# Start, end of the scan and entry to the feed-forward in another order; scan levels 0 to 7 as 64 by 64 blocks

## The reference

```
x = x + rmsnorm(concat(att, rec) @ w_out)      att: 8 query heads, 2 key heads, rope; rec: gated scan, 4 heads, 2 directions
x = x + rmsnorm(cross_attention(rmsnorm(x), rmsnorm(mem)) @ w_xo)
x = x + rmsnorm(conv_ffn(rmsnorm(x)))          width 2816, a convolution over 3 rows
x = x + rmsnorm((sig(ga) * (diff_attention @ A) + sig(gb) * (mla_attention @ B)) @ w_o)
x = x + rmsnorm((silu(h @ w_gate) * (h @ w_up)) @ w_down)
```

## Time and profile before

| | us |
|---|---|
| median of 3 runs | 932.08 (931.82 to 932.86) |
| the profiled execution | 931.06 |
| its span in the trace | 929.3 |
| PE busy | 896.8 |
| DVE busy | 616.0 |
| ACT busy | 479.0 |
| POOL busy | 79.9 |

### The profile page before, as it was taken

One profiled execution on the slowest core, in us unless ns is written; L12 is line 12 of the kernel. 1 busy time (PEld: TensorE's weight loads), 2 busy tenths in 40 slices (PEclk: granted clock), 3 DMA queues, 4 the chain that ended last, 5 costly groups with the idle time before them and its releaser, 6 DMA issues.

```text
span 929.3 us, 13932 instructions
## 1 busy us (share of the span) xinstructions
PE 896.8 (97%) x5540; PEld 794.2 (85%) x5540; DVE 616.0 (66%) x969; ACT 479.0 (52%) x841; POOL 79.9 (9%) x118
## 2 busy tenths in 40 slices
PE   5999899999989999999999999999999999999997
PEld 5988797889868999999878788788888789999996
DVE  5777977574668767668667747676787673654643
ACT  5844356564458346446535356675474672424331
POOL 1300200010020000000114210012011200000000
PEclk9999999999999999999999999999999999999999
DMA  9544324352538334655445455243255574564531
GB/s 339 188 136 148 124 92 163 109 204 95 181 128 300 136 137 145 217 183 194 170 148 185 177 181 182 73 164 139 91 187 176 168 262 136 176 204 165 181 137 45
DMA packets 91696, 152.56 MB, mean 164 GB/s; under 512 B 1968, under 2 KB 52272, under 8 KB 91376
## 3 DMA queue, kind: packets, MB, share of 16 engines
q1 hardware_dynamic: 91232, 150.94, 47.1%
...
q10 hardware_dynamic: 288, 0.47, 0.2%
...
## 4 chain that ended last, share of the span: by engine, by line
PE 81%; DVE 9%; ACT 4%; issue 3%; DMA 2%; POOL 0%; DVEq 0%; POOLq 0%; SPq 0%; ACTq 0%
PE ps L541 71%; DVE sb_wlo L2033 2%; DMA sb_ring<-in_w_in 2%; ACT sb_whi L1485 1%; PE ps L866 1%; PE ps L713 1%; PE ps L699 1%; PE ps L663 1%; PE ps L962 1%; PE ps L769 1%; PE ps L1137 1%; DMA sb_x<-in_x 1%; DVE sb_b L2186 1%; ACT sb_probs L1737 0%; DVE sb_b L2161 0%
## 5 line engine op out<-in xcount | busy, mean ns | idle before, releaser
L2033 DVE TENSOR_TENSOR sb_wlo<-sb_ring,sb_whi 128x1024 fp32r<-128x1024 f32 (+2 forms) x169 | 201.8, 1210 | 108.6 <-ACT sb_whi L1485 108.1
L1485 ACT ACTIVATE sb_whi<-sb_ring 128x1024 fp32r<-128x1024 f32 (+2 forms) x169 | 173.4, 1043 | 106.0 <-PE ps L541 99.5
L541 PE MATMUL ps<-sb_whi,sb_tbhi 128*128 128x512 f32 (+2 forms) x296 | 116.7, 394 | 2.8 <-DVE sb_wlo L2033 2.8
L541 PE MATMUL ps<-sb_whi,sb_tblo 128*128 128x512 f32 (+2 forms) x296 | 113.5, 383 | 0.0
L541 PE MATMUL ps<-sb_wlo,sb_tbhi 128*128 128x512 f32 (+2 forms) x296 | 113.5, 383 | 0.0
L541 PE MATMUL ps<-sb_whi,sb_tahi 128*128 128x512 f32 (+1 forms) x180 | 69.4, 386 | 0.7 <-DVE sb_wlo L2033 0.6
L541 PEld LDWEIGHTS ps<-sb_whi,sb_tbhi 128*128 128x128 f32 x296 | 55.7, 188 | 14.9 <-DVE sb_wlo L2033 4.6
L541 PE MATMUL ps<-sb_wlo,sb_tahi 128*128 128x512 f32 (+1 forms) x180 | 67.3, 374 | 0.0
L541 PE MATMUL ps<-sb_whi,sb_talo 128*128 128x512 f32 (+1 forms) x180 | 67.2, 374 | 0.0
L541 PEld LDWEIGHTS ps<-sb_whi,sb_tblo 128*128 128x128 f32 x296 | 55.6, 188 | 10.7
L541 PEld LDWEIGHTS ps<-sb_wlo,sb_tbhi 128*128 128x128 f32 x296 | 55.7, 188 | 9.2
...
## 6 DMA issues: line engine op xcount, KB each, us to landing
...
```

What stands on the lines that cost most here:

```text
L541: mm = pe.matmul(o, l[a_], r[b_], start=(start and n == 0), stop=(stop and n == 2), skip_group_check=not check)
L1485: act.activation(piece_pair(m)[0], src, ACT.Copy).then_inc(s("hi_done"), 1)
L2033: dve.tensor_tensor(low, pieces[m][1], high.bitcast(F32), ALU.subtract).then_inc(s("lo_done"), 1)
```

## The change

- **Beginning and pre_x_g.** Instead of the diagonal matrices DVE scales the rows themselves, in four instructions of 128x512, and PE transposes them (16 transposes). At the beginning POOL makes the inverse root of each row block apart, the four scalings are waited for in pairs of tiles, the first weight transfer holds 128 columns instead of 256, and PE first runs four matmuls on a zeroed buffer. The memory's norm scales in four instructions too.
- **Scan.** Levels 0 to 7 compute only the blocks on the diagonal of 64 by 64: 16 matmuls of 64x64 a level, the first half of the rows into PSUM partitions 0 to 63 and the second into 64 to 127. The kept matrix has 128x256 numbers a bank instead of 128x512, and so have the masked copies; the masks shrink from 896 to 384 columns. Level 7's block is the off-diagonal one; ACT puts it, and the compact matrix, in place in six copies after level 6 (which DVE waits for at level 8).
- **End of the scan.** DVE goes on to level 6 and 7 before the rotation of row block 0. The rotation of row block 1 (four products and two sums) moves to POOL.
- **Entry to the feed-forwards.** The low pieces stand before or behind the scalings in another order, the two scalings of row block 0 come together, the tiles of block 0 ahead of the squares of block 1.
- **Smaller ones.** POOL's inverse root per row block multiplies the first square in before the second is there. One or two low pieces move at three places (w_out's residual, "va0", the attentions' limit); in `attend` the values of head n-2 are taken before the other work, and `normalise_oa(1)` goes from n = 0 to n = 1. The load of one row of gains moves ahead by one chunk.

The diff, cut to its core:

```diff
-            def turn_norm(name, src):
-                pe.wait_ge(s(f"{name}_diag"), R)
+            def turn_norm(name):
+                pe.wait_ge(s(f"{name}_scaled"), 2 * R)
                 for m in range(4):
...
+                    turn(f"{name}.{m}", rows, [2 * m, 2 * m + 1], M[m], 2)
+            pe.wait_ge(s("blank"), 1)
+            for cols in (512, 512, 512, 256):
+                pe.matmul(bank[G[3]][:, 0:cols], probs[:, 0, 0:P], probs[:, 0, 0:cols], start=True, stop=True)
...
+            for r in range(R):
+                for m in range(4):
+                    if m % 2 == 0:
+                        pe.wait_ge(s("pre_mix_g_scaled"), 2 * r + m // 2 + 1)
...
-            def halves(T, h, head, r):
+            def halves(T, h, at):
...
-                        if n == 0:
-                            l, rhs = kdiag[:, at:at + P], hq[:, at:at + P]
-                        elif n < LEVELS:
-                            h = 1 << (n - 1)
-                            l, rhs = keys_at[n % 2][:, at:at + P], halves(QD, h, head, r)
...
+                        for a_ in range(2):
+                            block = slice(a_ * BLOCK, (a_ + 1) * BLOCK)
+                            own_at, other_at = at + a_ * BLOCK, at + (1 - a_) * BLOCK
+                            keys = kdiag if n == 0 else keys_at[n % 2]
+                            if n == 0:
+                                rhs = hq[:, own_at:own_at + BLOCK]
+                            elif n < LEVELS - 1:
+                                rhs = halves(QD, 1 << (n - 1), own_at)
+                            else:
+                                rhs = QD[:, (1 - a_) * NS + other_at:(1 - a_) * NS + other_at + BLOCK]
+                            mm = pe.matmul(bank[M[b]][block, j * BLOCK:(j + 1) * BLOCK], keys[:, own_at:own_at + BLOCK], rhs,
+                                           start=True, stop=True, skip_group_check=True)
...
+            pe.wait_ge(s("scan_blocks"), 2)
...
             def rstd_rows(name, r):
-                pool.wait_ge(s(f"{name}_sq"), 2 * (r + 1))
...
-                step(pool.tensor_tensor(m, m, more, ALU.add))
+                pool.wait_ge(s(f"{name}_sq"), 2 * r + 1)
                 step(pool.tensor_scalar(m, m, 1.0 / D, EPS, ALU.mult, ALU.add))
+                pool.wait_ge(s(f"{name}_sq"), 2 * (r + 1))
+                step(pool.tensor_scalar(m, more, 1.0 / D, m, ALU.mult, ALU.add))
...
+            z, t = qkv[:, 1, 0:640], rtmp[:, 640:1280]
+            zp, tp = (v.rearrange("p (i two) -> p i two", two=2) for v in (z, t))
+            for src, dst, tables in ((z, t, (tsq, tsk)), (z, z, (tcq, tck))):
+                for table, lo, n in zip(tables, (0, 512), (8, 2)):
+                    q = slice(lo, lo + 64 * n)
+                    pool.tensor_tensor(heads(dst[:, q]), heads(src[:, q]), table[:, 1:2, :].to_broadcast([P, n, 64]),
+                                       ALU.mult).then_inc(s("rope1_mul"), 1)
+            pool.wait_ge(s("rope1_mul"), 4)
+            for a_, b_ in ((0, 1), (1, 0)):
+                pool.tensor_tensor(zp[:, :, a_], zp[:, :, a_], tp[:, :, b_], ALU.add).then_inc(s("rope1_added"), 1)
...
+            for half in range(2):
+                for b in range(2):
+                    act.wait_ge(*banks.empty(f"level6.{b}"))
+                block = slice(half * BLOCK, (half + 1) * BLOCK)
+                act.activation(Adiag[block, :, block], Ablock[block, :, :], ACT.Copy).then_inc(s("scan_blocks"), 1)
...
-                        dve.copy_predicated(Adiag[:, 4 * b:4 * b + 4, :],
-                                            masks[:, n - 1:n, :].bitcast(I32).to_broadcast([P, 4, P]),
+                        dve.copy_predicated(Ablock[:, 4 * b:4 * b + 4, :],
+                                            masks[:, n - 1:n, :].bitcast(I32).to_broadcast([P, 4, BLOCK]),
...
             def next_level(n):
-                ahead(reached[f"level{n}"] + 1)
+                if n < 6:
+                    ahead(reached[f"level{n}"] + 1)
                 if 0 < n < LEVELS:
                     double_queries(n - 1)
-                keep_level(n)
+                if n != LEVELS - 1:
+                    keep_level(n)
+                if n >= 6:
+                    ahead(reached[f"level{n}"] + 1)
                 if n < LEVELS - 1:
                     double_keys(n)
...
             ahead(reached["level5"] + 2)
+            next_level(6)
+            ahead(reached["level6"] + 2)
             rope1_turn(0)
-            next_level(6)
+            ahead(reached["level6"] + 3)
+            next_level(7)
             rope1_scale(0)
-            rope1_turn(1)
-            next_level(7)
             rope1_scale(1)
...
-                ahead_of(q1, 3)
-                scaled(post, f"{q0}.0", 0, 0, loads)
                 ahead_of(q1, 4)
                 ahead_of(in0, 1)
+                scaled(post, f"{q0}.0", 0, 0, loads)
                 scaled(post, f"{q1}.0", 1, 0, loads)
                 added_rows(post, (f"{q0}.0", f"{q1}.0"), 0)
-                ahead_of(in0, 2)
                 norm_rows(norm, f"{post}_added", 0)
+                ahead_of(in0, 3)
                 for half in range(2):
                     tiles_lo(norm, T, gain, 0, half)
+                ahead_of(in0, 4)
+                ahead_of(in1, 1)
                 scaled(post, f"{q0}.1", 0, 1, loads)
-                ahead_of(in0, 4)
                 scaled(post, f"{q1}.1", 1, 1, loads)
-                ahead_of(in1, 1)
                 added_rows(post, (f"{q0}.1", f"{q1}.1"), 1)
...
+            ahead_of("va0", 1)
             take_gained("ckvT", ckvT, [0, 1], COL_KVA)
...
-                   {0: [(take_v, 1), (normalise_oa, 1)], 2: [(oaT_lo, 1)], 5: [(take_a, 0, 0)], 6: [(take_a, 0, 1)],
-                    9: [(take_a, 1, 0), (take_a, 1, 1)]})
+                   {0: [(take_v, 1)], 1: [(normalise_oa, 1)], 2: [(oaT_lo, 1)], 5: [(take_a, 0, 0)], 6: [(take_a, 0, 1)],
+                    9: [(take_a, 1, 0), (take_a, 1, 1)]}, pieces_of["w_proj_b_20"][0] + 2)
```

134 lines of the change are left out of this document (74 added, 60 removed).

## The result

The changed kernel takes 916.15 us (median of four runs, 915.11 to 916.60) against 931.95 for the kernel before in the same session: 15.8 us less, a ratio of 0.9827 (95% interval 0.9810 to 0.9844). The forecast was 919.4 us in a range of 914.5 to 926. The profiled execution took 915.11 us, its span is 913.3.

A forecast was written before the change was run, and what follows sets the result against it. PE was taken to set the time nearly everywhere, leaving its idle time, slow stretches and side work to win. Terms summed to 12.7 us: 918.4 for the profiled execution, 919.4 for the median, range 914.5 to 926.

The forecast's parts named there:

- the beginning: Scalings and 16 transposes instead of diagonal matrices at the start: 1.2 us won, ends 0.3 and 2.3.
- pre_x_g: Norm before cross-attention, 32 records become 16: 0.9 us won, ends 0.65 and 1.1, a 0.58 stall included.
- "va0": Two low pieces ahead of the wait at "va0" end 0.77 of idle: 0.8 us won, ends 0 and 0.9.
- the loop over the heads: PE's idle in 640 to 660, from head 1's row maximum and the taking: 1.0 us won, ends 0 and 2.2.
- The levels: Scan levels take PE 1.3 to 2.0 us each, said not to matter; DVE and ACT's ring loses 0.5 a level.
- The scan's end: Queries and copy before rotation bring level 7 and the transposes behind level 8 earlier: 4.5 us won, between 2.1 and 6.9.
- POOL and DVE wholly in a row: Rival: their work adds up, so the scan's end gives 2.1 instead of 4.5; 921.8 us, chance 0.17.
- The entries: Feed-forward entries: first wins 3.1 us, ends 2.3 and 4.1; second shares 0.9 with 456 to 474.
- The stretch of 456 to 474: Together with the second feed-forward entry, 0.9 us won, ends 0.3 and 2.0.
- POOL's step: POOL's first step of 0.28 us leaves four chains; at the very end worth 0.3 us for certain.
- The slower rival: Scan matmuls of 64 columns don't run side by side or carry fixed cost: 941 us at 0.17 a record, chance 0.05.
- The rival that half of each gain is taken by the next wait: At both entries, mla and other moved places, half the gain goes to the next wait: 924.5 us, chance 0.08.

The follow-up runs named there:

- e3: The changed kernel with each of the 16 matmuls of scan levels 0 to 7 issued twice: 917.93 us.
- e11: The changed kernel with pre_x_g again by diagonal matrices, 16 matmuls in 32 records instead of 16 transposes: 916.64 us.
- e6: The changed kernel with the earlier order on ACT and DVE at both feed-forward entries, POOL's shorter chain kept: 918.89 us.

## Why the prediction was right, step by step

**The sum, 12.7 us forecast, 16.0 in the traces.** The time is 3.3 us under the forecast because most terms were too small: the beginning by 1.1, pre_x_g by 0.9, the first entry by 0.6, "va0" by 0.3, the second entry and the loop over the heads together by 0.5, the scan by 0.1, and the end too large by 0.2. The low ends as listed add up to 5.95 us, not to 5.7, which moves the slow end from 926.4 to 926.1.

**The beginning, 1.2 forecast, 2.3 won.** The upper end. The four scalings took 0.44 us each for block 0 and 0.55 for block 1, more than my 0.37, but the inverse root of block 0 came at 7.12, and half of the transposes were done before that of block 1 mattered. The clock stood at its upper level, for which I had paid 0.6 us of doubt. The executions with a second half-clock stretch give 1.1 to 1.3 at the second weight piece and 0.7 to 0.9 from 33 us on. No run undoes the scalings, the inverse root per block or the smaller first transfer, so how the 2.3 us are shared among these is not shown.

**The levels, about 0.5 forecast, 2.7 won: the step that was wrong.** I wrote that 1.3 to 2.0 us a level didn't matter, since a period of 8.2 was held by DVE and ACT. e3 shows that this is so only from level 4 on; at levels 0 to 3 PE is the limit, and there a level's shorter matmuls count. Behind levels 0, 1, 2 and 3 the products are 0.7, 0.95, 0.6 and 0.5 us further ahead than before them, 2.45 us together with 0.3 given back in between. I had read the period and its ring late in the scan (8.2 us from level 5 to level 6, at 91.71 and 99.92), where PE waits, and carried it to the early levels, where the starts are 7.4 to 8.1 us apart. PE's busy time over several levels would have shown it; the window of the kernel before over levels 0 to 4:

```profile
53.00:87.00 34.00, 33.93 (x193) 29.61 (x192) 24.59 (x33) 13.01 (x19) 0.00 (x0) 1.00 0.33 115
```

**The scan's end, 4.5 forecast for the whole term, 1.9 from level 6 on.** The low end of this term was 2.1, and it was reached: the contention of POOL and DVE came as the rival had it. The first product behind level 7 is 3.4 us further ahead than the last before it (2.4 by the wait that is gone, 1.0 by the blocks), the clock that doesn't fall adds 1.4, and 2.9 were then lost in PE's two waits. That the sum over the scan (2.7 + 1.9 = 4.6) meets the 4.5 is chance: the levels gave 2 us more and the end 2 us less. The rival "POOL and DVE wholly in a row" forecast 124.6 for the transposes, and the trace has 119.79. Its mechanism was right and its size too large: POOL's work was done by 113.9, beside DVE's, with DVE slower by 4.2 us instead of by 5.7, and the queue before it was shorter by what the levels had won.

**pre_x_g, 0.9 forecast, 1.8 won.** 0.9 by the transposes (e11). The other 0.9 stands before them, where the low piece now goes ahead of the sums (0.58 of idle), which I had put inside the 0.9 instead of beside it. A wait of 0.67 for the first low tile, forecast as the tiles' pace, is there:

```profile
197.20 0.36 PE L542 MATMUL ps<-sb_tbhi,sb_whi 128*128 128x256 f32 x1 [0.67 <-DVE sb_tblo L2096]
...
268.73 0.66 PE L664 MATMUL ps<-sb_col,sb_b 128*128 128x128 f32 x4 [1.05 <-DVE sb_b L2457]
```

The second row is what is left of idle at the first entry.

**The entries, 3.1 and part of 0.9 forecast, 3.7 and 0.7 won; e6 has 3.0 and 0.7 for the order.** Right in place and size. Of five idle pieces one of 1.05 is left, the wait for the scaling of block 1.

**The small ones.** "va0" gave 1.1 for 0.8. The stretch of 456 to 474, which was to bring part of the 0.9, gave nothing: before and after (here 12.5 us earlier) the windows have the same idle time, and the products on both sides are 12.44 us ahead.

```profile
456.00:474.00 18.00, 16.51 (x76) 12.80 (x75) 14.76 (x25) 11.38 (x28) 3.95 (x9) 1.00 0.40 136
443.50:461.50 18.00, 16.48 (x76) 12.75 (x75) 14.67 (x25) 11.36 (x28) 5.47 (x9) 1.00 0.40 139
```

The second entry gave 0.7. The loop over the heads gave 1.7 (1.4 and 1.1 less 0.8 given back) for 1.0; both waits went, where I had counted on less than half. POOL's step gave 0.1 at the end for 0.3, the one term that I had called certain: with one step less, the first of them began 0.17 us behind ACT's last record instead of 0.08 and took 0.26 instead of 0.19, for which the runs give no reason.

**The slower rival** (64 columns at 0.13 us a record or more) is far off: 0.036 us. The rival that half of each gain is taken by the next wait did not come either, but for the scan's end.
